# A recurrent block in fp32: where the row of cumulated decay comes from, TensorE or DRAM

## The reference, cut to what matters

```
g      = -exp(A_log) * softplus(a + dt_bias)          # log decay, one number per position and head
G      = cumsum(g) inside a chunk
decay  = exp(where(j <= i, G[i] - G[j], -inf))        # one matrix per chunk
L      = strict lower part of (beta*k) k^T * decay
u, w   = solve (I + L) against [beta*v, beta*k*exp(G)]
A      = q k^T * decay
o, S   = recurrence over the chunks with u, w, A, exp(G)
```

## Time and profile before

| | us |
|---|---|
| median of 3 runs | 1410.64 |
| the three runs | 1412.6, 1410.64, 1410.37 |
| the profiled execution | 1410.36 |
| its span, first to last instruction | 1408.5 |
| TensorE busy (share of the span) | 1349.7 (96%) |
| VectorE busy | 802.0 (57%) |
| ScalarE busy | 581.4 (41%) |
| GpSimd busy | 259.2 (18%) |

### The profile page before, as it was taken

The page is one execution under the profiler, slowest core; times in us unless marked ns, Lnnn a source line. Parts: engine busy times, 40 slices in busy tenths (PEclk is TensorE's granted clock), DMA queues, the critical chain, the costliest instruction groups (busy, mean ns, idle before and its releaser), DMA issues.

```text
span 1408.5 us, 20293 instructions
## 1 busy us (share of the span) xinstructions
PE 1349.7 (96%) x6903; PEld 1069.8 (76%) x6903; DVE 802.0 (57%) x1658; ACT 581.4 (41%) x973; POOL 259.2 (18%) x485
## 2 busy tenths in 40 slices
PE   6899999999999999999899999999997999999998
PEld 4678778787787878888688888888885767677776
DVE  4657575575755743444456553465645788943532
ACT  4445354453534532223244432344444455454522
POOL 1124041240412300001400000000042623222200
PEclk8999999999999999999899999999998999999999
DMA  5132222322223223333223323433242212222211
GB/s 153 47 90 72 73 65 62 86 68 72 68 61 88 68 71 101 89 104 90 75 76 103 89 86 93 120 90 99 66 113 74 70 45 63 58 75 60 60 46 74
DMA packets 208503, 111.46 MB, mean 79 GB/s; under 512 B 6827, under 2 KB 206794, under 8 KB 208458
## 3 DMA queue, kind: packets, MB, share of 16 engines
q1 hardware_dynamic: 208073, 110.86, 27.8%
q0 software_dynamic: 384, 0.03, 0.0%
HBM read 108.75 MB, written 2.10 MB: 79 GB/s over the span
## 4 chain that ended last, share of the span: by engine, by line
PE 74%; DVE 14%; POOL 4%; issue 4%; ACT 3%; DMA 0%; POOLq 0%; DVEq 0%; ACTq 0%
PE gb L597 60%; POOL Ue L1977 2%; POOL elt L1974 2%; PE gd L955 2%; PE gb L1006 2%; PE gd L1006 2%; PE gd L934 2%; ACT whi L1021 1%; DVE selb L1822 1%; DVE kc L1614 1%; DVE wlo L1379 1%; DVE act_a L1414 1%; DVE small L1821 1%; PE gd L609 1%; PE gd L945 1%
## 5 line engine op out<-in xcount | busy, mean ns | idle before, releaser
L597 PE MATMUL gb<-act_a,whi 128*128 128x512 f32 x2800 | 967.0, 406 | 17.8 <-DVE wlo L1379 11.0
L597 PEld LDWEIGHTS gb<-act_a,whi 128*128 128x128 f32 x2800 | 528.4, 189 | 142.2 <-issue 14.0
L597 PE MATMUL gb<-act_a,wlo 128*128 128x512 f32 x1488 | 583.3, 392 | 0.0
L597 PEld LDWEIGHTS gb<-act_a,wlo 128*128 128x128 f32 x1488 | 282.2, 190 | 56.7 <-issue 4.1
L1379 DVE TENSOR_TENSOR wlo<-raw,whi 128x1024 fp32r<-128x1024 f32 x190 | 233.9, 1231 | 137.6 <-ACT whi L1021 137.0
L1021 ACT ACTIVATE whi<-raw 128x1024 fp32r<-128x1024 f32 x212 | 222.9, 1052 | 171.3 <-PE gb L597 141.5
L597 PE MATMUL gb<-act_b,whi 128*128 128x512 f32 x304 | 109.2, 389 | 0.0
L2066 POOL TENSOR_TENSOR wlo<-raw,whi 128x1024 fp32r<-128x1024 f32 x22 | 52.7, 2397 | 146.1 <-ACT whi L1021 146.1
L597 PEld LDWEIGHTS gb<-act_b,whi 128*128 128x128 f32 x304 | 57.1, 188 | 11.9
L2032 POOL TENSOR_TENSOR zs<-zs,ca 128x512 f32<-128x512 f32 x3 | 5.4, 1786 | 322.0 <-ACT ca L1024 322.0
L1987 POOL TENSOR_TENSOR rr<-ss,rr 128x4 f32<-128x4 f32 x8 | 1.6, 200 | 287.2 <-DVE ss L1582 287.2
(11 more groups left out here) (421 smaller groups left out, 1562.7 us busy)
## 6 DMA issues: line engine op xcount, KB each, us to landing
raw<-in_w_in_dram SPq DMA_DIRECT2D x103, 512.0 KB, 3.6
raw<-in_w_up_dram SPq DMA_DIRECT2D x44, 512.0 KB, 3.7
raw<-in_w_down_dram SPq DMA_DIRECT2D x16, 384.0 KB, 3.1
raw<-in_w_down_dram SPq DMA_DIRECT2D x16, 320.0 KB, 3.1
raw<-in_w_a_out_dram SPq DMA_DIRECT2D x8, 512.0 KB, 3.5
raw<-in_w_b_out_dram SPq DMA_DIRECT2D x8, 512.0 KB, 3.5
raw<-in_w_o_dram SPq DMA_DIRECT2D x8, 512.0 KB, 3.4
raw<-in_w_out_dram SPq DMA_DIRECT2D x8, 512.0 KB, 3.5
```

The source lines that it names most:

```text
L597: ins = pe.matmul(gb[:, b, :], l, r, start=(first and m == 0), stop=(last and m == len(todo) - 1))
```

## The change

From the second head on, the row of G is no longer made by TensorE. In the first turn TensorE transposes all 32 columns of G (8 heads by 4 chunks) at (2, 1), ScalarE copies them out of PSUM at (2, 2) into Lp, used as scratch, and SP stores them to a DRAM tensor g_dram (8 heads by 512). In the turns 1 to 7 SP loads row h of it, broadcast to 128 partitions, straight into dec, ahead of the load for unit 2 of that head, after the previous head's AT. VectorE's step 0 then subtracts in place. Head 0 keeps TensorE's step -1, now behind a wait for the copy, since both use bank 3.

```
+        g_dram = nc.dram_tensor("g_dram", (HEADS, T), F32)
...
             def head_loads(h):
                 for s in range(8):
+                    if s == 2 and not (isinstance(h, int) and h == 0):
+                        sp.wait_ge(lt_ready, 2 * h)
+                        sp.dma_start(flat(dec), g_dram[ds(h, 1), :].to_broadcast([P, T])).then_inc(g_landed, 16)
                     load(N_B + 8 * h + s, N_B + s, w_in_v[:, :, column(B_COLS[s] - 3 * P)])
...
             head_loads(0)
+            sp.wait_ge(g_rows, 1)
+            sp.dma_start(g_dram[:, :].rearrange("h (c i) -> (h c) i", c=TC),
+                         flat(Lp)[0:HEADS * TC, :]).then_inc(g_kept, 16)
+            sp.wait_ge(g_kept, 16)
...
# TensorE
-                        if (s, m) == ((3, 0) if peeled else (2, 3)):
+                        if peeled and (s, m) == (2, 1):
+                            pe.wait_ge(gcum_sb, 1)
+                            pe.transpose(gd[0:HEADS * TC, 3, 0:P], sm[:, 5, 0:HEADS * TC], ident[:]).then_inc(g_turned, 1)
+                        if peeled and (s, m) == (3, 0):
+                            pe.wait_ge(g_rows, 1)
                             step(-1, h)
...
# ScalarE
+                        if peeled and (s, m) == (2, 2):
+                            sc.wait_ge(g_turned, 1)
+                            sc.activation(flat(Lp)[0:HEADS * TC, :], gd[0:HEADS * TC, 3, 0:P], ACT.Copy).then_inc(g_rows, 1)
...
# VectorE
                 if g == 0:
-                    dve.wait_ge(gb_done, h + 1)
-                    link(dve.tensor_tensor(dec[:], bank(gd[:, 3, :]), wide(hc[:, C_G:C_G + TC]), ALU.subtract))
+                    if isinstance(h, int) and h == 0:
+                        dve.wait_ge(gb_done, 1)
+                        src = bank(gd[:, 3, :])
+                    else:
+                        dve.wait_ge(hc_ready, h + 1)
+                        dve.wait_ge(g_landed, 16 * h)
+                        src = dec[:]
+                    link(dve.tensor_tensor(dec[:], src, wide(hc[:, C_G:C_G + TC]), ALU.subtract))
...
                 elif g == 2:
...
+                    if isinstance(h, int) and h == 0:
+                        dve.wait_ge(g_kept, 16)
```

More of the change, by code:

```diff
@@ L355, in hybrid_block_kernel @@
         gb_done = sem("gb_done")
+        g_turned = sem("g_turned")
+        g_rows = sem("g_rows")
+        g_kept = sem("g_kept")
+        g_landed = sem("g_landed")
         arg_ready = sem("arg_ready")
```

## The result

| | before | after |
|---|---|---|
| median, 16 runs each | 1410.70 us | 1413.24 us |
| ratio, 95% interval | | 1.0017 (1.0009 to 1.0025) |
| profiled execution's span | 1408.5 us | 1410.9 us |

A second comparison of the same two kernels gave 1414.84 us against 1411.02, ratio 1.0024 (1.0014 to 1.0034). So the change is clear of noise and small: 0.17 to 0.24% slower. The forecast was 1411.2 with a range of 1408.6 to 1414.2 us, and "no change" as the likeliest; the median of the second comparison, 1414.84, lies outside that range. Single executions of one kernel differ by 3 to 5 us (1409.27 to 1413.49 before, 1412.15 to 1415.31 after), so a difference of 2.5 us is one between medians.

What follows compares the result with a forecast made beforehand. TensorE bounds the whole (74% of the chain), but other engines set 30.0 us of each 58.80 us head, where the passes lie. 0.0 + 0.6 + 0.1 = +0.7 us gave 1411.2 us, range 1408.6 to 1414.2.

Steps and rivals of the forecast that it cites:

- The removed passes are worth nothing at the end: TensorE, heads 1 to 7: 0.89 us less per head lies where other engines set the time; worth 0.
- the prediction's own sign of being wrong: Distance of two Rr near 57.9 us (passes did bound), or 59.2 us and more (GpSimd's hold or late row).
- the port: VectorE's subtraction from two SBUF inputs holds GpSimd's L1987 and L1988; L1497 +0.08 us per head, +0.6 in seven.
- the row's landing: VectorE at L1493 would wait if the broadcast took over 40 us; 1418 us at 41 us; chance 0.03.
- The rival in which they count in full: TensorE, seven heads: the removed passes shorten the whole by 6.2 us, to 1404.3 us; chance 0.08.
- The rival with both subtractions as one block: GpSimd stays out for L1493 and L1494; L1497 +0.44 us per head, +3.1 in seven, 1413.6 us; chance 0.13.
- The waits and queues added: VectorE's wait for the row and SP's loads, heads 1 to 7: row lands at about 136, wanted at 177.2; cost 0.
- Head 0: TensorE's transpose waits for the cumulated sums, L664 starts 0.05 us later; with ScalarE's copy +0.1 us in all.
- The sum: Whole kernel: 0.0 for removed passes, 0.6 for seven heads, 0.1 for head 0, together +0.7 us.
- the rival of the held GpSimd: GpSimd kept out through both VectorE subtractions, L1493 and L1494, in seven heads: 1413.6 us; chance 0.13.

Runs made afterwards that it cites:

- passes gone: Kernel before without TensorE's eight row passes in heads 1 to 7; VectorE takes a minimum with whatever lies in PSUM, no DMA; 1412.95 us, ratio 1.0013.
- subtraction early alone: The changed kernel with only VectorE's subtraction and mask moved up to (1, 0), ScalarE's order as it was; 1414.31 us, ratio 1.0024.

## Why the prediction was right, and what it missed

- **The removed passes are worth nothing at the end.** Right. The wait before unit 4 was to grow from 0.98 to 1.9 us; it grew to 2.02. The distance of two Rr didn't fall by 0.9 in any head. But the prediction's own sign of being wrong, a distance of 59.2 us and more, did come in two heads (60.01 and 59.92), and by neither of the two causes that it named for it, the port or the row's landing. The rival in which they count in full (1404.3 us) is refuted by all traces.
- **The port.** Right in mechanism and nearly in size. L1987 was to end 0.07 us after L1493 (it ends 0.07 after L1520), L1988 at 120.72 on a clock on which everything now comes 0.41 us later, thus 121.13 (121.10), and L1497 was to be +0.08 us late: +0.05. The Trainium skill's rule ("SBUF — State Buffer", section "Who interferes with whom") agrees: two SBUF inputs held GpSimd (0.58 us), the same instruction with PSUM as one input did not (0.20 us, passes gone). The rival with both subtractions as one block is refuted: GpSimd's first instruction ended at 119.57, 0.03 us after the mask had started.
- **The waits and queues added.** Right: the row lands 42 us ahead. SP stood 2.7 us once before the row's first load, for head 0's AT, where the prediction had no wait, but no split waited for its weights.
- **Head 0.** Right as far as the reasoning went: TensorE waits 0.90 us for the sums, and L664 came 4.28 us after the sums were ready (53.95 to 58.23) where it had been 4.23 (55.15 to 59.38), +0.05 as worked out. ScalarE's copy took 0.25 us and the wait for kc behind it fell from 0.52 to 0.37.
- **The sum.** Missed by its missing term. The prediction gave TensorE's longer standstill the price 0: "So without the eight passes it stands 0.98 + 0.89 = 1.87 us before 126.96, and leaves at the same moment." It leaves at the same moment, and in two of the seven loop heads the clock is at half right after. That is +1.18 and +1.09 us where the forecast had nothing. (The 1.6 us in head 0 stand against 1.2 us less at the start of the span; they can't be laid to the longer standstill, since head 0's was not longer.) The time (1413.24) is inside the range, and the direction of the small shift was right, but +0.7 was named and +2.5 measured. That is luck: the range reached so far up for the rival of the held GpSimd (1413.6 us), which didn't happen, and 1414.84 in the second comparison is outside. A small slip besides: 1410.36 + 0.7 and 0.3 for the profiled execution make 1411.3, not 1411.2.

The step that failed is this price of 0, and behind it a habit of thought: a wait on an engine that isn't the bound was taken for empty time. The page "TensorE: Matmul & The Clock Gate" of the Trainium skill, section "What's actually happening", says that the clock follows how busy the array has been lately. The runs agree for the loop heads: with 2.0 us of standstill two of seven heads have a stretch of half clock in each of four traces (the change twice, passes gone, subtraction early alone), with 0 to 1.24 us none in seven traces.

## What to carry to other kernels

Work taken off TensorE in a place where it waits anyway doesn't only win nothing: it lengthens the standstill, and the granted clock behind it may fall, so ask of each longer wait what TensorE's next microseconds are worth. Look for the excess by the period of a loop: a few turns that are longer by the same amount, with the others unchanged, are not a chain that grew. A value that comes early is worth something only if its consumers are moved as well; here the row from DRAM came with a gain once the subtraction and ScalarE's order followed it (1404.6 us).

## What wasn't expected of the hardware

- Not every standstill of 2.0 us is followed by half clock: in the loop it is two heads of seven, three apart (3 and 6, or 2 and 5), in the same code at the same place of the turn. What picks the head is open.
- The length of the standstill isn't all. In head 0 TensorE stands 3.0 to 3.1 us before unit 4 in all kernels; a stretch of half clock follows in both traces of the change and in that of the early subtraction alone, in none of the others. That is open too.
- Useless products can pay: with sixteen passes (1.95 us) per head the seven heads take 412.0 us, without them 414.3.
- A GpSimd instruction of 1.01 us, held by VectorE, took 1.45 us and ended 0.87 us after VectorE's release (121.10 against 120.23): 0.14 us of it seem to lie before the point at which it is held, 0.13 in the one of 0.20 us, and the rest runs after the release. This split is an estimate from these end times.
